# Expert outputs stored by indirect transfers of GpSimd instead of plain stores of SyncE, in a two-layer encoder trunk

## The chip, the cores and the metric

The kernel runs on one core of a Trainium2 chip. The metric is device time in microseconds (us) of one execution. Before the change it is 1436.44 us, the median of 3 runs (1435.87 to 1436.81). The trace shown here comes from one profiled execution that took 1436.07 us and whose instructions span 1434.3 us.

Engines by their short names: PE is TensorE, DVE VectorE, ACT ScalarE, POOL GpSimd, SP SyncE. SP, ACT and POOL also issue transfers. Transfers issued by SP go to DMA queue q1, those of POOL to queue q0, those of ACT to q10; all queues are served by the same 16 DMA engines.

## What is computed

Two layers. Each adds a token mixer to the residual, then a mixture of experts. Layer 0 mixes by a gated short convolution and a bidirectional RG-LRU behind one input projection, layer 1 by windowed attention. The part that the change touches is the mixture of experts (512 tokens, 1024 channels, 16 experts of width 512, 2 experts per token, all data float32):

```
def grouped_moe(h, router_w, router_bias, w_gate, w_up, w_down):
    scores = sigmoid(hf @ router_w)
    ...                       # best group of 4 experts, best 2 experts in it
    top_w = top_s / sum(top_s)
    slot_tok = full(cap, T).at[dest].set(tok)      # slots in blocks of 128 for one expert
    xs = hpad[slot_tok].reshape(n_blocks, 128, D)
    yb = (silu(xb @ w_gate[e]) * (xb @ w_up[e])) @ w_down[e]   # per block
    out = zeros(T + 1, D).at[slot_tok].add(yb * slot_w)
```

Each token takes 2 slots, so 1024 slots are taken in a layer. The in-projection of layer 0 is `z = h @ w_in`, 1024 by 2560.

## The kernel before

Every engine has its own hand-written list of instructions, joined by semaphores. There is no scheduler: what stands first in an engine's list runs first, and an instruction that waits holds up all behind it on that engine.

**In-projection of layer 0.** The weight is cut into five slabs of 128 x 8 x 512 (2 MB), loaded by SP with `load_in(g)`. PE makes 20 tiles of z, four per slab (`z_tile`). For slabs 1 to 4 the weight is split in two float32r parts: ACT copies half a slab (`high_in(g, half)`, line 800), DVE subtracts (`low_in`, line 1245), and PE multiplies (line 1743). Tiles 0 to 3 are copied by ACT from PSUM to one scratch tile, `u_in` (line 817), read by DVE's convolution `conv_b`. Tiles 4 to 11 are taken by ACT with `take_z` (line 829); both kinds count the semaphore `z_act`. Between them ACT runs the RG-LRU gates of four channel tiles j (lines 839 to 847), and DVE their products and scans (lines 1197 to 1213). ACT's order from j = 2 on is: gates, `take_z(9)`, square roots, `high_in(3, 0)`, then `take_z(10)` and the gates of j = 3.

Beside this, SP streams the modulation weights in slices of 512 KB through a ring of four (`load_mod`, line 426), which DVE sums (`mod_acc`, lines 1030 and 1032). SP's order in the middle of the stage is the rest of `load_mod(3)`, the slab `("out", 0)`, `load_in(3)`, `load_mod(4)`, `load_in(4)`.

**Memory for the experts' outputs.** `y_dram` has 23 blocks of 128 rows of 4 KB: 16 for the experts and 7 for blocks of experts that have over 128 tokens. The kernel before zeroes only the last 7, by POOL, early in the in-projection (lines 656 and 658).

**Expert stage, once per layer.** After routing, POOL gathers an expert's 128 token rows from `xn_dram` (lines 668 and 675), with an index column of `slot_tok`. An empty slot's index is past the bounds and its row is skipped. PE's step for expert e: first half of the gate product, transposes of the hidden rows of e - 1, second half, down product of e - 1 (line 1872), transposes of the input of e + 1 (line 1847), up product (lines 1861). DVE scales the down product of e - 1 into `ybuf` (`take_y`, line 1491), one of two buffers, and counts `yb_ready`. SP refills three weight slabs a step and then stores the whole `ybuf`, 128 rows, to `y_dram` (`store`, line 537). At the end come the blocks of experts with over 128 tokens (one in layer 0, two in layer 1, stored at line 576), and then POOL gathers every token's two rows of `y_dram` (line 719) and DVE adds them with their weights (`combine`).

Of the kernel before, what the change touches and what calls it, by code (L numbers as in the profile page):

```python
# [20 lines left out]
ALU = mybir.AluOpType  # L21
# [4 lines left out]
I32 = mybir.dt.int32  # L26
# [3 lines left out]
P = 128  # L30
# [4 lines left out]
HALF = 512  # L35
# [3 lines left out]
NE, NG, EPG = 16, 4, 4  # L39
FF = 512  # L40
FT = FF // P
MAX_OVER = 2 * S // P - 1
NBLK = NE + MAX_OVER
# [49 lines left out]
def build(nc, ctx, a, out):  # L93
    def small(name, shape, dt=F32):
        return ctx.enter_context(nc.sbuf_tensor(name, shape, dt))
# [28 lines left out]
    u_in = R[:, 0, :]  # L124
# [17 lines left out]
    ybuf = [R[:, 9:11, :].rearrange("p a n -> p (a n)"), R[:, 11:13, :].rearrange("p a n -> p (a n)")]  # L142
# [71 lines left out]
    empty = small("slot_empty", [P, WIDE])  # L214
    dst = small("dest", [P, 2, TT])
    info = small("over_info", [P, 8], I32)
    hot = small("hot_b", [P, TT, NE], BF16)
    idx = [small(f"gather_idx{i}", [P, 1], I32) for i in range(2)]

    xn_dram = nc.dram_tensor("xn_rows", [S, D], F32, kind="Internal").ap()  # L220
    y_dram = nc.dram_tensor("y_rows", [NBLK * P, D], F32, kind="Internal").ap()
# [24 lines left out]
    z_ready, z_act, z_dve = sem("z_ready"), sem("z_act"), sem("z_dve")  # L246
# [7 lines left out]
    xn_stored, place_ready, slots_summed, slots_ready = sem("xn_stored"), sem("place_ready"), sem("slots_summed"), sem("slots_ready")  # L254
# [160 lines left out]
    def _(sp):  # L415
# [94 lines left out]
        def stream_experts(l):  # L510
            e0 = l * NE

            free = {0: [(z_ready, 20), (mod_used, (MOD_SPLIT - 1) * MOD_SLICES + 4), (mod_used, MOD_SPLIT * MOD_SLICES), (y_ready, 8), (z_ready, 16), (y_ready, 8)],
                    1: [(av_ready, 8), (y_ready, 15), (y_ready, 16), (y_ready, 16), (y_ready, 16), (y_ready, 16)]}[l]
            for e in range(2):
                for c in range(3):
                    sp.wait_ge(*free[3 * e + c])
                    load_part(l, c, e, e)

            def refill(pair, par, more, first=False):  # L520

                e = 2 * pair + par
                if more:
                    sp.wait_ge(gate_done, e + (e0 + 1))
                    load_part(l, 0, e + 2, par)
                if not first:
                    sp.wait_ge(down_done, e + e0)
                    load_part(l, 2, e + 1, 1 - par)
                if more:
                    sp.wait_ge(up_done, e + (e0 + 1))  # L530
                    load_part(l, 1, e + 2, par)
                if not first:
                    store(e - 1, 1 - par)

            def store(e, par):
                sp.wait_ge(yb_ready, e + (e0 + 1))
                sp.dma_start(y_dram[bass.ds(e * P, P), :], ybuf[par]).then_inc(yb_stored[par], 16)

            refill(0, 0, True, first=True)
            refill(0, 1, True)  # L540
            with sp.Fori(1, NE // 2 - 1) as i:
                refill(i, 0, True)
                refill(i, 1, True)

            refill(NE // 2 - 1, 0, False)
            o = over[l]
            n_over = sp.value_load(info[0:1, 7:8], min_val=0, max_val=MAX_OVER)

            def load_over(k, name, c):
                ex = sp.value_load(info[0:1, bass.ds(k, 1)], min_val=0, max_val=NE - 1)  # L550
                sp.dma_start(part_dst(c, 0), part_src(l, c, ex)).then_inc(o[name], 16)

            sp.wait_ge(gate_done, e0 + NE - 1)
            sp.wait_ge(up_done, e0 + NE - 1)
            with sp.If(n_over > 0):
                load_over(0, "wg", 0)
                load_over(0, "wu", 1)
            sp.wait_ge(down_done, e0 + NE - 1)
            with sp.If(n_over > 0):
                load_over(0, "wd", 2)  # L560
                sp.sem_inc(o["stored"], 16)
            store(NE - 2, 0)
            if l == 0:
                for w, used in enumerate((gate_done, up_done, down_done)):
                    sp.wait_ge(used, e0 + NE)
                    load_slab(("qkv", w), w_qkv[:, :, w * HALF:(w + 1) * HALF])
            store(NE - 1, 1)
            with sp.Fori(0, MAX_OVER) as k:
                with sp.If(k + 1 < n_over):
                    ex = sp.value_load(info[0:1, bass.ds(k + 1, 1)], min_val=0, max_val=NE - 1)  # L570
                    for c, name, used in ((0, "wg", "gate"), (1, "wu", "gu"), (2, "wd", "down")):
                        sp.wait_ge(o[used], k + 1)
                        sp.dma_start(part_dst(c, 0), part_src(l, c, ex)).then_inc(o[name], 16)
                with sp.If(k < n_over):
                    sp.wait_ge(o["yb"], k + 1)
                    sp.dma_start(y_dram[bass.ds((k + NE) * P, P), :], ybuf[0]).then_inc(o["stored"], 16)
                    sp.wait_ge(o["stored"], (k + 2) * 16)
                    sp.sem_inc(turn_seen, 1)
            for par in range(2):
                sp.wait_ge(yb_stored[par], 16 * (NE // 2) * (l + 1))  # L580
# [32 lines left out]
    def _(gp):  # L613
# [18 lines left out]
        link(gp.iota(tok1[:, :], [[P, TT]], base=1, channel_multiplier=1, allow_small_or_imprecise_dtypes=True))  # L632
        link(gp.iota(b_id[:, :], [[1, WIDE]], base=0, channel_multiplier=0, allow_small_or_imprecise_dtypes=True))
        link(gp.iota(p_id[:, :], [[1, P]], base=0, channel_multiplier=0, allow_small_or_imprecise_dtypes=True))
        link(gp.memset(gpad[:, :, :], NEG))
        gp.sem_inc(consts_ready, 1)

# [19 lines left out]
        for b in range(NE, NBLK):  # L657
            gp.dma_start(y_dram[b * P:(b + 1) * P, :], zeros).then_inc(y_zeroed, 16)

        def gathers(l):  # L660
            e0 = l * NE
            gp.wait_ge(xn_ready, 4 * (2 * l + 2))
            link(gp.memset(R[:, 0:4, :], 0.0))
            gp.wait_ge(slots_ready, 2 * l + 1)
            gp.wait_ge(xn_stored, 16 * TT * (l + 1))

            def gather_first(buf, done):
# [9 lines left out]
                                      bounds_check=S - 1, oob_is_err=False).then_inc(done, 16)  # L677

            gather_first(0, xs_filled[0])
            gp.wait_ge(slots_ready, 2 * l + 2)  # L680
            gather_first(1, xs_filled[1])
            with gp.Fori(0, NE // 2 - 1) as i:
                link.enter_loop(i, 0, 2)
                for par in range(2):
                    gp.wait_ge(xs_turned, 2 * i + (par + e0 + 1))
                    gp.sem_inc(turn_seen, 1)
                    gather(2 * i + (par + 2), par, xs_filled[par])
                link.leave_loop(0, NE // 2 - 1)

            o = over[l]  # L690
            gp.wait_ge(route_ready, l + 1)
# [3 lines left out]
            def gather_over(k):  # L695
                gp.tensor_copy(idx[0][:, :], slot_tok[:, bass.ds(k + NE, 1)]).then_inc(o["step"], 1)
                gp.wait_ge(o["step"], k + 1)
                gp.sem_inc(turn_seen, 1)
                gp.indirect_dma_start(out=xs[0], out_offset=None, in_=xn_dram,
                                      in_offset=bass.IndirectOffsetOnAxis(ap=idx[0][:, 0:1], axis=0),  # L700
                                      bounds_check=S - 1, oob_is_err=False).then_inc(o["xs"], 16)

            with gp.If(n_over > 0):
                gather_over(0)
            with gp.Fori(0, MAX_OVER - 1) as k:
                with gp.If(k + 1 < n_over):
                    gp.wait_ge(o["turned"], k + 1)
                    gp.sem_inc(turn_seen, 1)
                    gather_over(k + 1)
# [309 lines left out]
    def _(v):  # L1019
# [337 lines left out]
        def place_first(l):  # L1357

            v.wait_ge(rank_ready, l + 1)
            link(stt(first_rank[:, :], hot[:, :, 0], -float(PAST), v3(ps[:, 1, 0:n])[:, :, 0], ALU.mult, ALU.add))  # L1360
            link(ts(first_rank[:, :], first_rank[:, :], float(PAST), None, ALU.add))
            tt_(first_hot, p_id[:, :].unsqueeze(1).to_broadcast([P, TT, P]), first_rank[:, :].unsqueeze(2).to_broadcast([P, TT, P]), ALU.is_equal).then_inc(place_ready, 1)
            v.wait_ge(slots_summed, 2 * l + 1)
            found = ps[:, 2, 0:1]
            link(ts(empty[:, 0:1], found, 0.0, float(NO_TOKEN), ALU.is_equal, ALU.mult))
            stt(slot_tok[:, 0:1], found, -1.0, empty[:, 0:1], ALU.add, ALU.add).then_inc(slots_ready, 1)
            v.wait_ge(slots_ready, 2 * l + 1)

        def route(l):

# [29 lines left out]
            slots = ps[:, 2, 1:WIDE]  # L1400
            link(ts(empty[:, 1:WIDE], slots, 0.0, float(NO_TOKEN), ALU.is_equal, ALU.mult))
            stt(slot_tok[:, 1:WIDE], slots, -1.0, empty[:, 1:WIDE], ALU.add, ALU.add).then_inc(slots_ready, 1)
            v.wait_ge(slots_ready, 2 * l + 2)

        def route_rest(l):

# [668 lines left out]
```

## Time and profile before

| | |
|---|---|
| median of 3 runs | 1436.44 us (1435.87 to 1436.81) |
| profiled execution | 1436.07 us, span 1434.3 us, mean granted PE clock 0.938 |
| PE busy | 1260.2 us, 88% of the span |
| DVE busy | 950.0 us, 66% |
| ACT busy | 616.9 us, 43% |
| POOL busy | 169.5 us, 12% |
| bytes moved | 353.14 MB, mean 246 GB/s |
| of these on queue q1 (SP) | 327.28 MB |
| of these on queue q0 (POOL) | 20.46 MB |

A share of busy time is a mean over stages with different limits, so the table alone does not say which engine sets the time at a given place. The chain of waits does: it starts at the last instruction and goes back, at each step, to what released it. A time in the views counts from the span's start.

### The profile page before, as it was taken

To read this page: it belongs to the slowest core of one execution; us is meant where nothing else is said; L and a number is where in the kernel's file an instruction comes from. 1 tells how busy PE (TensorE), PEld (TensorE's weight loads), DVE (VectorE), ACT (ScalarE), POOL (GpSimd) and SP (SyncE) were. 2 spreads that over 40 slices of the span, in tenths; PEclk is the share of its full clock that TensorE was granted. 3 is DMA by queue.
4 is the path that set the end of the run, shared out by engine and by line. 5 is a ranking of instruction groups with operands and counts; after the bars stand their busy time and mean duration, and the time that the engine had idled before them with its cause. 6 is when DMAs were issued, how large, how long until landed. Compare 5 with 4: busy or idle time off the path is not lost.

```text
span 1434.3 us, 14569 instructions
## 1 busy us (share of the span) xinstructions
PE 1260.2 (88%) x4997; PEld 853.9 (60%) x4997; DVE 950.0 (66%) x1331; ACT 616.9 (43%) x792; POOL 169.5 (12%) x177
## 2 busy tenths in 40 slices
PE   2999899948999999983999999999489999999881
PEld 2566665546666666741788854467367666667430
DVE  8678876467777777613866587856577777776114
ACT  3486301335555555402422167634255555554001
POOL 6100000010000000002000047710110000000002
PEclk9999899969999999997899999999599999999996
DMA  9836674257999999883375230023679999998445
GB/s 353 325 115 239 223 287 152 95 204 296 369 365 369 364 380 378 304 313 132 125 285 177 88 118 1 1 74 130 241 295 377 375 366 368 376 367 305 146 181 190
DMA packets 79552, 353.14 MB, mean 246 GB/s; under 512 B 12632, under 2 KB 12816, under 8 KB 70544
## 3 DMA queue, kind: packets, MB, share of 16 engines
q1 hardware_dynamic: 67616, 327.28, 61.7%
q0 software_dynamic: 8352, 20.46, 4.0%
q10 hardware_dynamic: 3536, 4.79, 0.9%
q8 instruction: 27, 0.44, 0.1%
q14 instruction: 21, 0.17, 0.0%
HBM read 334.15 MB, written 28.31 MB: 253 GB/s over the span
## 4 chain that ended last, share of the span: by engine, by line
PE 77%; DVE 11%; DMA 5%; ACT 3%; issue 3%; POOL 1%; SPq 0%; DVEq 0%; ACTq 0%; POOLq 0%
PE ps L1861 24%; PE ps L1872 17%; PE ps L1960 9%; PE ps L1781 4%; PE ps L1852 3%; PE ps L1743 3%; PE ps L1788 2%; PE ps L1847 2%; PE ps L1748 2%; DVE scratch L1032 2%; PE ps L2004 2%; PE ps L2032 2%; PE ps L2018 2%; DMA x_res<-in_x_dram 1%; PE ps L1866 1%
## 5 line engine op out<-in xcount | busy, mean ns | idle before, releaser
L1872 PE MATMUL ps<-slab_ring,scratch 128*128 128x512 f32 x560 | 246.5, 593 | 3.4 <-ACT scratch L940 2.1
L1861 PE MATMUL ps<-slab_ring_r,gate_rows_r 128*128 128x512 f32 x512 | 202.0, 394 | 0.0
L1872 PEld LDWEIGHTS ps<-slab_ring,scratch 128*128 128x128 f32 x560 | 105.8, 190 | 124.2 <-issue 117.3
L1453 DVE TENSOR_TENSOR slab_ring_r<-slab_ring,h_t_r 128x2048 fp32r<-128x2048 f32 x64 | 143.9, 2288 | 17.1 <-ACT h_t_r L862 17.1
L1960 PE MATMUL ps<-slab_ring_r 128*128 128x512 f32 x384 | 121.8, 399 | 1.8 <-DVE h_t_r L1089 1.8
L1861 PE MATMUL ps<-h_t_r,gate_rows_r 128*128 128x512 f32 x256 | 106.1, 414 | 14.8 <-DVE scratch_r L1487 7.6
L862 ACT ACTIVATE h_t_r<-slab_ring 128x2048 fp32r<-128x2048 f32 x64 | 118.7, 1902 | 0.0
L1861 PEld LDWEIGHTS ps<-slab_ring_r,gate_rows_r 128*128 128x128 f32 x512 | 98.2, 192 | 19.2 <-issue 0.5
L891 ACT ACTIVATE scratch<-ps,mod_ab 128x128 f32<-128x128 f32 x128 | 48.2, 457 | 136.2 <-PE ps L1847 136.2
L1861 PE MATMUL ps<-h_t_r,scratch_r 128*128 128x512 f32 x256 | 102.3, 400 | 0.0
L1453 DVE TENSOR_TENSOR slab_ring_r<-slab_ring,x_norm_r 128x2048 fp32r<-128x2048 f32 x32 | 73.3, 2293 | 41.3 <-ACT x_norm_r L862 41.3
L1453 DVE TENSOR_TENSOR slab_ring_r<-slab_ring,mod_ring_r 128x2048 fp32r<-128x2048 f32 x32 | 73.3, 2292 | 41.1 <-ACT mod_ring_r L862 41.1
L727 POOL TENSOR_SCALAR mod_ring<-mod_ring,row_rcp 128x512 f32<-128x512 f32 x48 | 77.0, 1616 | 185.7 <-DVE row_rcp L1634 185.7
L1960 PEld LDWEIGHTS ps<-slab_ring_r 128*128 128x128 f32 x384 | 72.8, 191 | 19.1 <-issue 2.9
L862 ACT ACTIVATE x_norm_r<-slab_ring 128x2048 fp32r<-128x2048 f32 x32 | 61.1, 1911 | 46.7 <-PE ps L1861 46.6
L862 ACT ACTIVATE mod_ring_r<-slab_ring 128x2048 fp32r<-128x2048 f32 x32 | 61.1, 1911 | 46.7 <-PE ps L1861 46.6
L1491 DVE TENSOR_TENSOR scratch<-ps,gate_rows 128x512 f32<-128x512 f32 x70 | 45.1, 686 | 53.9 <-PE ps L1872 53.0
L1743 PE MATMUL ps<-slab_ring_r,h_t_r 128*128 128x512 f32 x192 | 68.8, 436 | 9.7 <-DVE slab_ring_r L1245 9.7
L1960 PE MATMUL ps<-slab_ring_r,h_t_r 128*128 128x512 f32 x192 | 75.7, 395 | 0.0
L1032 DVE SCALAR_TENSOR_TENSOR scratch<-slab_ring,c_silu,scratch 128x1024 f32<-128x1024 f32 x49 | 69.1, 1410 | 3.8 <-DMA slab_ring<-in_mod_w_dram 2.2
L1861 PEld LDWEIGHTS ps<-h_t_r,gate_rows_r 128*128 128x128 f32 x256 | 49.8, 195 | 25.7 <-issue 16.4
L1743 PE MATMUL ps<-slab_ring_r 128*128 128x512 f32 x192 | 64.5, 415 | 0.0
(329 smaller groups left out, 2225.4 us busy)
## 6 DMA issues: line engine op xcount, KB each, us to landing
slab_ring<-in_expert_w_gate_dram SPq DMA_DIRECT2D x35, 2048.0 KB, 9.6
slab_ring<-in_expert_w_up_dram SPq DMA_DIRECT2D x35, 2048.0 KB, 10.1
slab_ring<-in_expert_w_down_dram SPq DMA_DIRECT2D x35, 2048.0 KB, 9.6
mod_ring<-in_mod_w_dram SPq DMA_DIRECT2D x40, 512.0 KB, 4.7
y_rows<-scratch SPq DMA_DIRECT2D x35, 512.0 KB, 10.2
slab_ring<-in_mod_w_dram SPq DMA_DIRECT2D x32, 512.0 KB, 4.7
slab_ring<-in_mod_w_dram SPq DMA_DIRECT2D x12, 1024.0 KB, 11.4
slab_ring<-in_w_qkv_dram SPq DMA_DIRECT2D x6, 2048.0 KB, 11.9
```

The costliest lines, as they stand in the source:

```text
L727: gp.tensor_scalar(prob[n % 8], prob[n % 8], rsum[:, n:n + 1], None, ALU.mult).then_inc(scaled_pool, 1)
L862: act.activation(top, w, ACT.Copy).then_inc(high_ready[c], 1)
L891: ins = act.activation(xsT[par][:, kt, :], ps[:, 0, kt * P:(kt + 1) * P], ACT.Identity, bias=AB[:, s, 1, kt:kt + 1], scale=AB[:, s, 0, kt: ...
L1032: ins = stt(dest, w, cs[:, m:m + 1], dest, ALU.mult, ALU.add)
L1453: tt_(rest, w, top.bitcast(F32), ALU.subtract).then_inc(low_ready[c], 1)
L1491: ins = tt_(buf[:, h * HALF:h * HALF + HALF], ps[:, 5 + h, :], G[:, 2 * l + 1, h * HALF:h * HALF + HALF], ALU.mult)
L1743: ins = pe.matmul(ps[:, z_bank(t), :], w[:, kt, cut], x[:, kt, :], start=(kt == 0 and i == 0), stop=(kt == KT - 1 and i == 2))
L1781: ins = pe.matmul(ps[:, 2 * t + half, :], mixT[:, kt, cut], slab(("out", half))[:, kt, :], start=(i == 0), stop=(i == KT - 1))
L1852: ins = pe.matmul(ps[:, bank, :], xsT[0][:, kt, :], w[:, kt, :], start=(kt == 0), stop=(kt == KT - 1))
L1861: ins = pe.matmul(ps[:, bank, :], x, w, start=(kt == 0 and i == 0), stop=(kt == KT - 1 and i == 2))
L1872: ins = pe.matmul(ps[:, 5 + h, :], hidT[:, f, :], w[:, 2 * f + h, :], start=(f == 0), stop=(f == FT - 1))
L1960: ins = pe.matmul(ps[:, i % 6, :], x[:, kt, cut], y[:, k, :], start=(kt == 0 and n == 0), stop=(kt == KT - 1 and n == 2))
```

## The change

Three things change.

POOL now also zeroes the 16 experts' blocks of `y_dram`, once, after its 7 old zero stores: it waits until `z_act` has reached 9 (the four copies to `u_in` and `take_z` of tiles 4 to 8), clears `u_in`, and issues 32 transfers of 128 rows x 2 KB (256 KB) from it. The expert stage of layer 0 begins only when all of them have landed.

The routing on DVE writes one more small tile, `y_slot`: the row number of each slot, or a number past the bounds for an empty slot. `slots_ready` counts three a layer instead of two, and POOL's second gather waits for the third.

SP's `store` is gone. POOL issues an indirect transfer of `ybuf` for each expert instead (`scatter`): a copy of one index column, then the transfer, in which the rows of empty slots are skipped. The stores of the extra blocks stay with SP.

```diff
@@ smalls
+    y_base = small("y_base", [P, NE])
+    y_slot = small("y_slot", [P, NE], I32)
+    y_idx = [small(f"store_idx{i}", [P, 1], I32) for i in range(2)]
@@ SP, stream_experts
-                if not first:
-                    store(e - 1, 1 - par)
-
-            def store(e, par):
-                sp.wait_ge(yb_ready, e + (e0 + 1))
-                sp.dma_start(y_dram[bass.ds(e * P, P), :], ybuf[par]).then_inc(yb_stored[par], 16)
...
-            store(NE - 2, 0)
...
-            store(NE - 1, 1)
@@ POOL, constants
+        link(gp.iota(y_base[:, :], [[P, NE]], base=0, channel_multiplier=1, allow_small_or_imprecise_dtypes=True))
@@ POOL, after the 7 old zero stores
+        gp.wait_ge(z_act, 9)
+        link(gp.memset(u_in, 0.0))
+        for b in range(NE):
+            for h in range(2):
+                gp.dma_start(y_dram[b * P:(b + 1) * P, h * HALF:(h + 1) * HALF], u_in).then_inc(y_zeroed, 16)
@@ POOL, gathers(l)
+            if l == 0:
+                gp.wait_ge(y_zeroed, 16 * (MAX_OVER + 2 * NE))
...
-            gp.wait_ge(slots_ready, 2 * l + 2)
+            gp.wait_ge(slots_ready, 3 * l + 3)
             gather_first(1, xs_filled[1])
-            with gp.Fori(0, NE // 2 - 1) as i:
-                link.enter_loop(i, 0, 2)
+
+            def scatter(e, ready, buf):
+                gp.wait_ge(yb_ready, ready)
+                gp.sem_inc(turn_seen, 1)
+                link(gp.tensor_copy(y_idx[buf][:, :], y_slot[:, bass.ds(e, 1)]))
+                gp.sem_inc(turn_seen, 1)
+                gp.indirect_dma_start(out=y_dram, out_offset=bass.IndirectOffsetOnAxis(ap=y_idx[buf][:, 0:1], axis=0), in_=ybuf[buf],
+                                      in_offset=None, bounds_check=NBLK * P - 1, oob_is_err=False).then_inc(yb_stored[buf], 16)
+
+            for par in range(2):
+                gp.wait_ge(xs_turned, par + e0 + 1)
+                gp.sem_inc(turn_seen, 1)
+                gather(par + 2, par, xs_filled[par])
+            with gp.Fori(1, NE // 2 - 1) as i:
+                link.enter_loop(i, 1, 4)
                 for par in range(2):
                     gp.wait_ge(xs_turned, 2 * i + (par + e0 + 1))
                     gp.sem_inc(turn_seen, 1)
                     gather(2 * i + (par + 2), par, xs_filled[par])
+                    scatter(2 * i + (par - 2), 2 * i + (par + e0 - 1), par)
...
+            scatter(NE - 4, e0 + NE - 3, 0)
@@ POOL, after the first gather of an extra block
+            for e in range(NE - 3, NE):
+                scatter(e, e0 + e + 1, e % 2)
@@ DVE, end of route(l)
+            tt_(y_slot[:, :], y_base[:, :], empty[:, 0:NE], ALU.add).then_inc(slots_ready, 1)
+            v.wait_ge(slots_ready, 3 * l + 3)
```

The list of POOL around the zero stores, in the kernel before (`x_norm` is the zeroed tile of the old stores, `scratch` in line 663 the buffers of the gathers):

```order
L656 MEMSET x_norm 128x1024 [waits pool_step,xn_turned]
L658 DMA y_rows<-x_norm 128x1024 [waits pool_step]
L658 DMA y_rows<-x_norm 128x1024 x6
L663 MEMSET scratch 128x2048 [waits xn_ready]
L668 DMA scratch<-xn_rows,slot_token 128x1024 [waits xn_stored,slots_ready,pool_step]
```

The same place in the changed kernel (`scratch` in lines 657 and 660 is `u_in`):

```order
L652 MEMSET x_norm 128x1024 [waits pool_step,xn_turned]
L654 DMA y_rows<-x_norm 128x1024 [waits pool_step]
L654 DMA y_rows<-x_norm 128x1024 x6
L657 MEMSET scratch 128x512 [waits z_act]
L660 DMA y_rows<-scratch 128x512 [waits pool_step]
L660 DMA y_rows<-scratch 128x512 x31
L667 MEMSET scratch 128x2048 [waits xn_ready,y_zeroed]
L672 DMA scratch<-xn_rows,slot_token 128x1024 [waits xn_stored,slots_ready,pool_step]
```

One memset and 32 transfers stand between the old zero stores and the first instruction of the expert stage.

The list of POOL in the loop over pairs of experts, changed kernel, the first expert of a pair:

```order
L677 ISA [waits xs_turned]
L677 COPY gather_idx<-slot_token 128x1
L70 ISA
L679 DMA scratch<-xn_rows,gather_idx 128x1024 [waits pool_step]
L688 REGISTER_ALU
L690 ISA [waits yb_ready]
L690 COPY store_idx<-y_slot 128x1
L70 REGISTER_ALU
L692 DMA y_rows<-scratch,store_idx 2944x1024 [waits pool_step]
```

The wait for `yb_ready` and the store stand behind the gather of the same step. SP's list in the same loop lost its wait for `yb_ready` and the store; before, it read:

```order
L445 DMA slab_ring<-in_expert_w_gate_dram 128x4096
L445 ISA [waits down_done]
L445 DMA slab_ring<-in_expert_w_down_dram 128x4x1024
L445 DMA slab_ring<-in_expert_w_up_dram 128x4096 [waits up_done]
L537 ISA [waits yb_ready]
L537 DMA y_rows<-scratch 128x1024
```

The three weight loads stay as they were and in the same order.

## Rows read from the trace of the kernel before

**Rows 1.** The chain that ended last: share of the span by engine.
```profile
PE 77%; DVE 11%; DMA 5%; ACT 3%; issue 3%; POOL 1%; SPq 0%; DVEq 0%; ACTq 0%; POOLq 0%
```

**Rows 2.** The same chain in time, one expert step: start us, us, what.
```profile
346.18 8.20 PE ps L1861 x36
...
354.82 2.75 PE ps L1861 x12
357.56 6.87 PE ps L1872 x16
365.32 8.20 PE ps L1861 x36
```

**Rows 3.** The same chain, in-projection.
```profile
119.96 1.30 DVE scratch L1032
...
122.12 15.00 DMA slab_ring<-in_w_in_ab_dram
137.17 1.79 issue
138.96 0.58 ACT x_norm L829
...
158.33 2.30 DVE slab_ring_r L1245
160.63 0.14 issue
160.77 13.95 PE ps L1743 x48
```

**Rows 4.** ACT in time, in-projection: start us, us, instruction [idle before <-releaser].
```profile
112.03 0.58 ACT L829 ACTIVATE x_norm<-ps 128x512 f32<-128x512 f32 x1
...
137.15 1.91 ACT L800 ACTIVATE h_t_r<-slab_ring 128x2048 fp32r<-128x2048 f32 x1 [7.40 <-DMA slab_ring<-in_w_in_ab_dram]
...
160.47 1.91 ACT L800 ACTIVATE h_t_r<-slab_ring 128x2048 fp32r<-128x2048 f32 x1 [7.12 <-DMA slab_ring<-in_w_in_ab_dram]
```

**Rows 5.** DVE in time, same stretch.
```profile
139.16 2.29 DVE L1245 TENSOR_TENSOR slab_ring_r<-slab_ring,h_t_r 128x2048 fp32r<-128x2048 f32 x1 [2.53 <-ACT h_t_r L800]
141.37 0.75 DVE L1030 TENSOR_SCALAR scratch<-mod_ring,c_silu 128x1024 f32<-128x1024 f32 x1
...
173.89 2.29 DVE L1245 TENSOR_TENSOR slab_ring_r<-slab_ring,h_t_r 128x2048 fp32r<-128x2048 f32 x1
```

**Rows 6.** SP's DMA issues in time, same stretch.
```profile
121.27 0.33 SPq L426 DMA_DIRECT2D mod_ring<-in_mod_w_dram  x1
121.64 0.43 SPq L417 DMA_DIRECT2D slab_ring<-in_w_out_ab_dram  x1
122.12 0.59 SPq L417 DMA_DIRECT2D slab_ring<-in_w_in_ab_dram  x1
```

**Rows 7.** DMA traffic of 112 to 118 us, then of 124 to 130 us.
```profile
DMA packets 411, 1.49 MB, mean 248 GB/s; under 512 B 48, under 2 KB 48, under 8 KB 411
...
DMA packets 1163, 2.39 MB, mean 398 GB/s; under 512 B 32, under 2 KB 32, under 8 KB 1163
```

**Rows 8.** POOL in time: its memset and seven zero stores.
```profile
41.09 0.95 POOL L656 MEMSET x_norm<- 128x1024 f32 x1 [15.49 <-PE ps L1712]
42.36 3.93 POOL L658 DMA_DIRECT2D y_rows<-x_norm  x7 [0.32 <-POOL x_norm L656]
```

**Rows 9.** DMA queues of 48 to 54 us (packets, MB, share), and a load issued there.
```profile
q0 software_dynamic: 312, 1.15, 50.5%
q1 hardware_dynamic: 321, 1.18, 50.3%
...
slab_ring<-in_w_in_ab_dram SPq DMA_DIRECT2D x1, 2048.0 KB, 18.4
```

**Rows 10.** The same kind of load, issued in 148 to 154 us.
```profile
slab_ring<-in_w_in_ab_dram SPq DMA_DIRECT2D x1, 2048.0 KB, 8.6
```

**Rows 11.** POOL in time: gathers in the expert loop, then two later transfer issues.
```profile
346.44 0.18 POOL L673 COPY gather_idx<-slot_token 128x1 int32 x1 [22.72 <-PE ps L1847]
347.48 1.02 POOL L675 DMA_INDIRECT scratch<-xn_rows,gather_idx  x1 [0.85 <-POOL gather_idx L673]
365.57 0.19 POOL L673 COPY gather_idx<-slot_token 128x1 int32 x1 [17.07 <-PE ps L1847]
...
666.46 1.89 POOL L719 DMA_INDIRECT mod_ring<-y_rows,y_row  x1 [0.30 <-issue]
```

**Rows 12.** All stores of line 537: duration ns, first and last start us.
```profile
L537 SPq DMA_DIRECT2D y_rows<-scratch x32: 342/356/1792, 352.1 to 1346.5; - x32
```

**Rows 13.** DVE in time, end of the routing of layer 0.
```profile
307.79 0.18 DVE L1402 SCALAR_TENSOR_TENSOR slot_token<-ps,slot_empty 128x23 int32<-128x23 f32 x1
309.39 1.36 DVE L1481 TENSOR_SCALAR scratch<-ps,mod_ab 128x128 f32<-128x128 f32 x4 [1.42 <-PE ps L1847]
```

More of the change, by code:

```diff
@@ L658, in _ @@
             gp.dma_start(y_dram[b * P:(b + 1) * P, :], zeros).then_inc(y_zeroed, 16)
+        gp.wait_ge(z_act, 9)
[3 more added lines that the diff above has]
+                gp.dma_start(y_dram[b * P:(b + 1) * P, h * HALF:(h + 1) * HALF], u_in).then_inc(y_zeroed, 16)
         def gathers(l):
             e0 = l * NE
+            if l == 0:
+                gp.wait_ge(y_zeroed, 16 * (MAX_OVER + 2 * NE))
             gp.wait_ge(xn_ready, 4 * (2 * l + 2))
             link(gp.memset(R[:, 0:4, :], 0.0))
-            gp.wait_ge(slots_ready, 2 * l + 1)
+            gp.wait_ge(slots_ready, 3 * l + 1)
             gp.wait_ge(xn_stored, 16 * TT * (l + 1))
@@ L687, in gathers @@
                     gather(2 * i + (par + 2), par, xs_filled[par])
-                link.leave_loop(0, NE // 2 - 1)
+                    scatter(2 * i + (par - 2), 2 * i + (par + e0 - 1), par)
+                link.leave_loop(1, NE // 2 - 1)
+            scatter(NE - 4, e0 + NE - 3, 0)
             o = over[l]
@@ L1366, in place_first @@
             stt(slot_tok[:, 0:1], found, -1.0, empty[:, 0:1], ALU.add, ALU.add).then_inc(slots_ready, 1)
-            v.wait_ge(slots_ready, 2 * l + 1)
+            v.wait_ge(slots_ready, 3 * l + 1)
         def route(l):
@@ L1402, in route @@
             stt(slot_tok[:, 1:WIDE], slots, -1.0, empty[:, 1:WIDE], ALU.add, ALU.add).then_inc(slots_ready, 1)
-            v.wait_ge(slots_ready, 2 * l + 2)
+            tt_(y_slot[:, :], y_base[:, :], empty[:, 0:NE], ALU.add).then_inc(slots_ready, 1)
+            v.wait_ge(slots_ready, 3 * l + 3)
         def route_rest(l):
```

## Prediction

> **What bounds the kernel now.** I read the chain of waits first, by engine: PE holds 77% of it, DMA 5% [rows 1]. In time, the expert loop is PE alone: a step goes from 346.18 to 365.32 us, 19.1 us, and in it the chain names only PE lines [rows 2]. No transfer, not the weights and not the stores of line 537, stands in the chain there. 14 steps of each layer look like this. So what the change takes off the DMA engines in the loop pays only if something waits for them, and nothing does.
>
> Then I read the stage into which the new zero stores are put. Here a transfer does stand in the chain: slab 3 of the in-projection is issued at 122.12 us, and the chain waits 15.00 us for it [rows 3]. ACT sat idle for 7.40 us before its copy of that slab at 137.15 us [rows 4]. ACT runs in order, so `take_z(10)` (138.96 us) and the gates of j = 3 stand behind that copy; behind these come DVE's scans, DVE's second split of slab 3 at 158.33 us, and PE's tiles at 160.77 us, from which PE runs on [rows 3]. DVE waited 2.53 us for the same copy [rows 5]. Nothing on this path has slack: if slab 3 lands later, all of it moves.
>
> **The zero stores: when.** `take_z(8)` is ACT's row at 112.03 us, 0.58 us long, so `z_act` is 9 at 112.6 us [rows 4]. A memset of 128x1024 took 0.95 us and the first store followed 0.3 us later [rows 8]; half the size makes about 0.5 us, so the first zero store is issued at 113.5 us. Seven stores took 3.93 us to issue, 0.56 us each [rows 8]; 32 take 18 us, until 131.5 us. They carry 32 x 0.262 = 8.39 MB. Issued at 0.47 MB a us, they come faster than the 0.39 to 0.40 MB a us that the DMA engines move when full (398 GB/s [rows 7]), so q0 has a backlog throughout.
>
> **What a backlog on q0 does to q1.** The trace of before shows it once, while the seven old zero stores run: from 48 to 54 us q0 moved 312 packets and q1 321, each for half of the engines' time [rows 9]. So the queues take turns packet by packet. A 2 MB slab issued then took 18.4 us to land [rows 9]; one issued at 151.8 us, with q0 empty, took 8.6 us [rows 10].
>
> The Trainium skill, page "DMA: Bandwidth & Descriptors", section "Where 436 GB/s comes from", gives about 358 GB/s as the limit between HBM and one core's SBUF. The trace shows 398 GB/s with loads alone. By the page's figure the same bytes as below would cost 4.45 / 0.358 = 12.4 us, 1.3 us more than I take.
>
> **The sum.** By 121.27 us, when slab 3's group of loads begins [rows 6], the DMA engines can move 7.8 us x 0.40 = 3.1 MB; q1 has about 1.0 of the 1.49 MB of its 112 to 118 us left to move [rows 7], so 2.1 MB of zeros are done and 6.3 MB wait. Ahead of slab 3's landing, q1 has a modulation slice (0.52 MB), the slab `("out", 0)` (2.10 MB) and slab 3 itself (2.10 MB) [rows 6], 4.7 MB: at 0.39 MB a us that is 12.1 us, and with some 3 us of start and landing it is the 15.9 us from 121.27 to 137.15. So q1 is near first in, first out. Turn by turn, each 2 KB packet of the two slabs lets one 2 KB packet of zeros pass (4.19 MB) and each 4 KB packet of the slice one of 2 KB (0.26 MB): 4.45 MB, less than the 6.3 MB that wait. At 0.40 MB a us: **+11.1 us** on the landing of slab 3, from 137.1 to about 148 us, and on everything behind.
>
> Bounds of this term: if the zeros that wait all go first, 6.3 / 0.39 = 16.2 us. If POOL issues as slowly as its slowest issue in the trace, 1.89 us [rows 11], zeros come at 0.262 / 1.89 = 0.139 MB a us; q1 then has 0.26 MB a us and its 4.7 MB take 18.1 instead of 12.1 us: +6.0 us. I take 11.1, which rests on the nearest rows, the same kind of store by the same engine in the same stage [rows 8, 9].
>
> After slab 3 has landed, about 1.9 MB of zeros are left, beside the four slices that follow. The first three of these are needed at 141.37, 142.1 and 143.4 us plus 11 [rows 5]: 1.57 MB of slices and 0.8 MB of zeros take 5.9 us from the slab's last packet at about 146.3 us, and with 2 us of landing the third slice is there at 154.2, needed at 154.5: nothing. The zeros end near 157 us. Slab 4, issued at 151.8 us before, is issued 11 us later too, at 163, with q0 empty again. Its copy on ACT (160.47 us [rows 4]) feeds a DVE instruction at 173.89 us [rows 5], 11.5 us of slack after the copy's 1.91 us. Both slabs together therefore cost one delay. The expert stage's new wait for all zero stores is over more than 130 us before POOL reaches it: its first gather is near 300 us, hidden by the rest of the in-projection and the out-projection.
>
> **The loop.** SP loses 32 issues of 0.36 us [rows 12] and q1 loses 32 x 0.52 = 16.8 MB; at most 8.4 MB come back on q0, since of a layer's 2048 rows at most 1024 are taken. Worth nothing where PE alone is in the chain. POOL gains per step a copy (0.18 us), 0.85 us and an issue of 1.02 us, as its gather costs [rows 11]: 2.1 us out of 17.07 us idle. The new wait for `yb_ready` stands behind the gather of the same step. Only the next gather is queued behind it, 19 us later, and the awaited count is reached before: `take_y(e - 2)` follows the down product that PE does just before the transposes that release the gather. If that cover were gone, 2.1 us x 28 would be the price. `ybuf` is needed again two steps later, 38 us, against a landing of some 10 us. Nothing.
>
> **Routing.** One DVE instruction of about 0.18 us behind the row at 307.79; DVE then idles 1.42 us for PE [rows 13]. It delays POOL's second gather by 0.2 us, whose rows PE needs 11 us later. Nothing, in either layer. In the tails the stores of experts 14 and 15 were and are out of the chain; the last extra block's store and the gathers that follow are unchanged.
>
> Sum: 1436.07 + 11.1 = **1447.2 us** for the profiled execution; the median of before is 0.37 us above that execution, within its runs' spread of 0.94 us.
>
> **The rivals.**
>
> A, POOL's issue is slow. The Trainium skill, page "DMA: Bandwidth & Descriptors", section "SWDGE vs HWDGE vs iDMA", says that GpSimd writes its descriptors to SBUF and is locked out while VectorE is in a two-port mode. The mechanism in rows: 1.89 us an issue instead of 0.56 [rows 8, 11], with DVE nearly full in 113 to 131 us. The price is the lower bound above, +6.0 us, 1442.1. Against it: the seven stores beside a busy DVE took 0.56 us each.
>
> B, more than turn by turn. The zeros that wait go first (+16.2), or the slices behind slab 3 come late and DVE waits for them too: 1449.5 to 1453. For it: 2 KB writes to HBM at this density are in no row.
>
> C, hidden anyway. SP's loads are served first, or slab 3's delay stays under 3 us: 1436 to 1439. Against it: the half and half of [rows 9].
>
> D, the other side. The loop waits for DMA in a way that the chain does not name, and fewer bytes help. If the loop were bound by bytes, 8.4 MB less at 0.37 MB a us would give 22.7 us back, which against 11.1 makes 1424.5. It decides from 11.1 / 28 = 0.4 us a step. Against it: every step is 19.1 us, all on PE, with no idle time named [rows 2].
>
> That the rows of empty slots are moved after all would not matter, as nothing waits for the loop's stores.
>
> **How the numbers follow.** Forecast 0.62 (own range 1444.5 to 1449.5), A 0.14, B 0.12, C 0.09, D 0.03. A measurement of this kernel can tell 0.2%, 2.9 us, from no change. Slower by more than that: forecast, A and B, 0.88. Within: C, 0.09. Faster: D, 0.03. The range 1441 to 1452.5 takes in A and most of B and leaves out C, D and the end of B.
>
> **What would show it.** ACT's copy of slab 3 starts near 148 us instead of 137.15, with some 18 us idle before it on the transfer. From 113.5 us q0 and q1 share the DMA engines near 1:1 in packets until about 157 us. PE's tile row of 160.77 us stands near 172, and the offset then stays at 11 us to the end. The expert step is still 19.1 us. If slab 3 lands before 141 us, the term is wrong. If the offset grows or shrinks after 172 us, I have missed a wait or a gain; if a step of the loop changes by over 0.1 us, the loop was not PE's alone.

## Result: 0.94% slower, and the profile after

| | before | changed |
|---|---|---|
| median of 4 runs, same chip | 1436.15 us (1434.85 to 1436.81) | 1448.95 us (1448.75 to 1451.38) |
| ratio | | 1.0094 (95% interval 1.0082 to 1.0107) |
| profiled execution, its span | 1436.07, 1434.3 us | 1449.06, 1447.3 us |
| bytes moved | 353.14 MB | 353.04 MB |
| of these on q1 (SP) | 327.28 MB | 310.50 MB |
| of these on q0 (POOL) | 20.46 MB | 37.14 MB |

The forecast was 1447.2 us, range 1441 to 1452.5. The bytes moved are the same before and after, within 0.1 MB: 16.8 MB of full stores left q1, and 8.4 MB of zeros and 8.3 MB of indirect stores came to q0.

The chain of waits of the changed kernel, in-projection (start us, us, what; it answers to [rows 3]; lines of the changed kernel are some 20 higher):

```profile
122.91 27.79 DMA slab_ring<-in_w_in_ab_dram
...
152.54 0.58 ACT x_norm L850
...
171.90 2.30 DVE slab_ring_r L1266
174.20 0.14 issue
174.34 13.84 PE ps L1765 x48
```

Slab 3 was 27.8 us in flight instead of 15.0, and every row behind it stands 13.6 us later: `take_z(10)` at 152.54 instead of 138.96, PE's tiles at 174.34 instead of 160.77. ACT in time shows the wait itself (to be laid beside [rows 4]), and DVE's row beside that of [rows 5]:

```profile
150.72 1.91 ACT L821 ACTIVATE h_t_r<-slab_ring 128x2048 fp32r<-128x2048 f32 x1 [21.10 <-DMA slab_ring<-in_w_in_ab_dram]
...
174.05 1.91 ACT L821 ACTIVATE h_t_r<-slab_ring 128x2048 fp32r<-128x2048 f32 x1 [7.13 <-DMA slab_ring<-in_w_in_ab_dram]
```

```profile
152.74 2.29 DVE L1266 TENSOR_TENSOR slab_ring_r<-slab_ring,h_t_r 128x2048 fp32r<-128x2048 f32 x1 [14.82 <-ACT h_t_r L821]
```

The wait for slab 3 grew from 7.40 to 21.10 us. The wait for slab 4, in the second row, stayed at 7.1 us, since it was issued that much later too. POOL in time shows the zero stores (compare [rows 8]):

```profile
112.54 0.53 POOL L657 MEMSET scratch<- 128x512 f32 x1 [66.09 <-ACT x_norm L850]
113.36 11.20 POOL L660 DMA_DIRECT2D y_rows<-scratch  x21 [0.30 <-POOL scratch L657]
138.94 5.87 POOL L660 DMA_DIRECT2D y_rows<-scratch  x11 [14.37 <-issue]
```

The first is issued at 113.36 us, 0.53 us each, but POOL stops for 14.37 us after the 21st. And the traffic while slab 3 was under way, from 121.5 us to its landing at 150.7 us (packets, MB, share):

```profile
q1 hardware_dynamic: 2601, 6.12, 53.8%
q0 software_dynamic: 1634, 5.36, 49.1%
```

5.36 MB of zeros passed. In the kernel before, q1 moved 5.54 MB in its 15.6 us of that kind, alone. The two shares near one half are a mean over four unlike stretches, in each of which the engines were full:

| stretch, us | q0: packets, MB | q1: packets, MB | what happens |
|---|---|---|---|
| 121.5 to 126 | 481, 1.57 | 5, 0.02 | zeros alone |
| 126 to 135.4 | 628, 2.04 | 668, 1.59 | turns |
| 135.4 to 142.6 | 26, 0.07 | 1384, 2.81 | loads alone, after POOL's pause |
| 142.6 to 150.7 | 499, 1.68 | 544, 1.71 | turns |

The expert loop, in the chain (it answers to [rows 2]):

```profile
359.43 8.20 PE ps L1883 x36
368.06 2.77 PE ps L1883 x12
370.83 6.87 PE ps L1894 x16
378.59 8.20 PE ps L1883 x36
```

A step is 19.16 us, as before. The indirect stores beside it, and POOL in time:

```profile
L692 POOL DMA_INDIRECT y_rows<-scratch,store_idx x32: 971/1026/1909, 362.9 to 1360.9; - x32
...
DMA to landing us min/median/max: 3.2/9.3/11.9
```

```profile
359.70 0.18 POOL L677 COPY gather_idx<-slot_token 128x1 int32 x1 [22.77 <-PE ps L1869]
360.74 1.02 POOL L679 DMA_INDIRECT scratch<-xn_rows,gather_idx  x1 [0.86 <-POOL gather_idx L677]
361.76 0.20 POOL L690 COPY store_idx<-y_slot 128x1 int32 x1
362.92 1.02 POOL L692 DMA_INDIRECT y_rows<-scratch,store_idx  x1 [0.96 <-POOL store_idx L690]
```

They land within 11.9 us, against 38 us until `ybuf` is needed again.

### The profile page after: what moved, and what is told of

Same layout as the page of the kernel before. It is cut to its first block, busy times and chain, and to the rows that moved or that the text cites. A ratio compares the mean times of both kernels' runs of the same rounds, so it can differ in the third digit from the quotient of the medians.

```text
span 1447.3 us, 14737 instructions
## 1 busy us (share of the span) xinstructions
PE 1259.5 (87%) x4997; PEld 852.2 (59%) x4997; DVE 945.3 (65%) x1333; ACT 616.6 (43%) x792; POOL 245.5 (17%) x275
## 2 busy tenths in 40 slices
DMA packets 82113, 353.04 MB, mean 244 GB/s; under 512 B 15220, under 2 KB 15404, under 8 KB 73104
## 3 DMA queue, kind: packets, MB, share of 16 engines
q1 hardware_dynamic: 63008, 310.50, 57.8%
q0 software_dynamic: 15520, 37.14, 7.0%
## 4 chain that ended last, share of the span: by engine, by line
PE 77%; DVE 10%; DMA 6%; ACT 3%; issue 2%; POOL 1%; SPq 0%; DVEq 0%; POOLq 0%; ACTq 0%
PE ps L1883 24%; PE ps L1894 17%; PE ps L1982 8%; PE ps L1765 4%; PE ps L1803 4%; PE ps L1874 3%; PE ps L1810 2%; PE ps L1869 2%; PE ps L1770 2%; DMA slab_ring<-in_w_in_ab_dram 2%; PE ps L2026 2%; PE ps L2054 2%; PE ps L2040 2%; DVE scratch L1053 2%; DMA x_res<-in_x_dram 1%
## 5 line engine op out<-in xcount | busy, mean ns | idle before, releaser
L1982 PE MATMUL ps<-slab_ring_r 128*128 128x512 f32 x384 | 121.1, 397 | 2.9 <-DVE h_t_r L1110 2.9
L677 POOL COPY gather_idx<-slot_token 128x1 int32 (+1 forms) x28 | 5.2, 185 | 377.1 <-PE ps L1869 377.1
```

The costliest lines, as they stand in the source:

```text
L1982: ins = pe.matmul(ps[:, i % 6, :], x[:, kt, cut], y[:, k, :], start=(kt == 0 and n == 0), stop=(kt == KT - 1 and n == 2))
```

## The experiments

Two theories go through all of them. T: the cost is slab 3's later landing, because zeros on q0 and loads on q1 take turns at the DMA engines. S: part of it comes from the indirect stores or the routing. Others are named where they enter. Each ratio is to runs of the kernel before on the same chip.

**e2, the zeros without the rest.** The kernel before, with POOL's memset, its 32 stores and the wait for them; SP still stores the outputs.

```diff
+        gp.wait_ge(z_act, 9)
+        link(gp.memset(u_in, 0.0))
+        ...                       # 32 stores, as in the change
         def gathers(l):
+            if l == 0:
+                gp.wait_ge(y_zeroed, 16 * (MAX_OVER + 2 * NE))
```

> The kernel before plus the 32 zero stores at the changed kernel's place; SP still stores the outputs. Theory T (the zeros cost all, by taking turns with slab 3's load): 1449, within 1.5 us of the changed kernel, ACT's copy of slab 3 near 150.7 us. Rival S (part of the 13 us comes from the indirect stores or the routing): below 1447.

Measured 1450.98 us, ratio 1.0093 (1.0077 to 1.0108), the changed kernel's own ratio. The zeros alone make the whole cost; S falls.

**e3, the rest without the cost of the zeros.**

```diff
-        gp.wait_ge(z_act, 9)
+        gp.wait_ge(z_ready, 20)
```

> The changed kernel with the zero stores held until the last tile of the in-projection (z_ready 20, some 205 us), where the DMA engines are half idle. Theory T: the delay is gone, 1436.2 within 1.5 us; this is then also what the indirect stores alone are worth, nothing. Rival D (fewer bytes in the expert loop help): 1433 or less. Rival S: above 1438.

Measured 1436.75 us against 1437.00, ratio 0.9995 (0.9986 to 1.0004). ACT's copy of slab 3 is back:

```profile
137.15 1.91 ACT L821 ACTIVATE h_t_r<-slab_ring 128x2048 fp32r<-128x2048 f32 x1 [7.14 <-DMA slab_ring<-in_w_in_ab_dram]
```

So the place makes the cost: the same 8.4 MB cost nothing here. The indirect stores are worth nothing that can be measured, in either direction, to within some 0.1%.

**e4, the zeros earlier.** They begin when the last convolution has read `u_in`, 35 us sooner.

```diff
-        gp.wait_ge(z_act, 9)
+        gp.wait_ge(y_zeroed, 16 * MAX_OVER)
+        gp.wait_ge(xr_ready, LRU_TILES)
```

> The changed kernel with the zero stores begun as soon as the last convolution has read u_in (xr_ready 4, some 77.5 us), 35 us earlier. DMA engines moved about 140 GB/s from 80 to 120 us before, so 8.4 MB fit before slab 3's loads at 121 us, POOL's pause included. Theory T: 1436 to 1438. If the cost were tied to the stores and not to slab 3: 1449.

Measured 1436.54 us against 1435.68, ratio 1.0004 (0.9995 to 1.0014), as T has it. POOL's pause of 14.43 us after 21 stores is there as well and costs nothing.

**e5, the zeros just behind slab 3.**

```diff
-        gp.wait_ge(z_act, 9)
+        gp.wait_ge(weight_high, 5)
```

> The changed kernel with the zero stores held until ACT has copied the first half of slab 3 (some 139 us, 26 us later than in the changed kernel). The backlog then meets slab 4, which has 11.5 us of slack. Theory T (turns): slab 4 lands 6 to 7 us later, inside the slack: 1436 to 1438.5. Rival V (zeros that wait go first): slab 4 lands 14 us later, 1439 or more.

Measured 1439.67 us, ratio 1.0022 (1.0012 to 1.0032). Slab 4 did as T says: its copy starts at 167.56 instead of 160.47 us, 7.1 us later and not 14, inside its slack. So V falls here, though the time alone would fit it:

```profile
167.56 1.92 ACT L821 ACTIVATE h_t_r<-slab_ring 128x2048 fp32r<-128x2048 f32 x1 [14.27 <-DMA slab_ring<-in_w_in_ab_dram]
```

The time lies above T's range all the same, for a reason that neither theory had. DVE waits for modulation slices:

```profile
168.91 0.75 DVE L1051 TENSOR_SCALAR scratch<-mod_ring,c_silu 128x1024 f32<-128x1024 f32 x1 [1.34 <-DMA mod_ring<-in_mod_w_dram]
170.87 1.29 DVE L1053 SCALAR_TENSOR_TENSOR scratch<-mod_ring,c_silu,scratch 128x1024 f32<-128x1024 f32 x1 [1.21 <-DMA mod_ring<-in_mod_w_dram]
173.22 1.28 DVE L1053 SCALAR_TENSOR_TENSOR scratch<-mod_ring,c_silu,scratch 128x1024 f32<-128x1024 f32 x1 [1.06 <-DMA mod_ring<-in_mod_w_dram]
```

These three add to 3.6 us, and the chain of this run goes through such a slice (issued at 163.11 us, 10.0 us in flight). I had given slack to slab 4 and none of my attention to the slices that stand behind it in q1.

**e6, half the dose.**

```diff
         for b in range(NE):
+            if b == NE // 2:
+                gp.wait_ge(z_ready, 20)
             for h in range(2):
```

> The changed kernel with 16 of the 32 zero stores at their place and 16 held until 205 us. About 2 of the 4.2 MB are moved before slab 3's group of loads begins; the rest passes before slab 3 lands, by T and V alike: 2.1 / 0.40 = 5 us, 1441.5. If the cost came from POOL's pause in issuing (it stopped after 21 of 32) and not from bytes, it would be gone: 1436.

Measured 1440.69 us, ratio 1.0029 (1.0017 to 1.0040). Slab 3's copy starts at 142.83 us, 5.7 us late, with no pause among the 16 stores at that place; the span is 3.7 us longer than before, less than the 5 expected, so 2 us were regained behind it. The cost is there without a pause beside slab 3, so it does not come from the pause.

**e8, twice the dose.**

```diff
-        for b in range(NE):
+        for b in list(range(NE)) * 2:
```

> The changed kernel with the zeroing done twice, 64 stores instead of 32, all at the same place. Theory T (turns while slab 3 loads): slab 3 lands at most some 2 us later than in the changed kernel, and slab 4 is slowed inside its slack: 1449 to 1453. Rival V (all zeros that wait go first): 14.7 MB ahead of slab 3, 1470 or more.

Measured 1450.99 us, ratio 1.0102 (1.0076 to 1.0127). Slab 3's copy starts at 152.40 us, 1.7 us later than in the changed kernel, for 8.4 MB more. Two things bound the delay. POOL pauses after the same 21 stores, so most of the added zeros are not yet issued while slab 3 loads; the 14.7 MB of the expectation could not stand ahead of it. And from 142.6 us on, when zeros are issued again, the queues take turns (635 packets on q0 and 645 on q1 until 152.4 us). Had the 28 stores that POOL issues from 138.29 us on gone first, their 7.3 MB at 0.41 MB a us would have held slab 3 up by some 18 us, by my estimate. So zeros first (V), part of rival B, falls for loads that are already under way. For the start of the loads it does not: see the part on the prediction.

**e9, half the descriptor memory.**

```diff
-    nc = _bacc.Bacc("TRN2", target_bir_lowering=False, num_devices=1, dynamic_dma_scratch_size=4096)
+    nc = _bacc.Bacc("TRN2", target_bir_lowering=False, num_devices=1, dynamic_dma_scratch_size=2048)
```

> The changed kernel with half the memory for POOL's transfer descriptors (2048 instead of 4096). If the pause after 21 stores is the full descriptor memory (28 stores with the 7 old ones, 9 descriptors a store and DMA engine, 252 of 256), POOL now pauses after 7 of the 32 (14 with the old ones). Fewer zeros wait when slab 3's loads begin: by T 1440 to 1447. If the pause has another cause, it stays after 21 and the time at 1449.

Measured 1445.47 us, ratio 1.0067 (1.0051 to 1.0084). POOL pauses as expected, and slab 3's copy starts at 146.44 us:

```profile
113.93 3.75 POOL L660 DMA_DIRECT2D y_rows<-scratch  x7 [0.30 <-POOL scratch L657]
124.20 7.63 POOL L660 DMA_DIRECT2D y_rows<-scratch  x14 [6.52 <-issue]
146.01 6.04 POOL L660 DMA_DIRECT2D y_rows<-scratch  x11 [14.19 <-issue]
```

The doses give one line. The MB are those of q0 from 121.5 us to the start of slab 3's copy:

| | zeros that passed | slab 3's copy later by | MB a us |
|---|---|---|---|
| e6, half | 2.39 MB | 5.7 us | 0.42 |
| e9, half the descriptor memory | 3.85 MB | 9.3 us | 0.41 |
| changed kernel | 5.36 MB | 13.6 us | 0.39 |
| e2, zeros alone | 5.90 MB | 14.6 us | 0.41 |
| e8, double | 6.15 MB | 15.3 us | 0.40 |

A megabyte of zeros in slab 3's way costs 2.4 to 2.5 us, whatever changes the number of megabytes. (The stage begins up to 0.7 us later in some of these runs than in the kernel before; with that taken off it is 2.3 to 2.6 us.) The last column is the rate of full DMA engines, 0.40 MB a us. So the line says that bytes in the way make the delay; it does not say by what rule the queues share.

**e10, slab 3 out of the way of the zeros.** The changed kernel, with SP's order altered:

```diff
-        load_mod(3)
-        sp.wait_ge(z_ready, 4)
-        load_slab(("out", 0), w_out[:, :, 0:HALF])
+        load_mod(3, range(6))
         sp.wait_ge(z_ready, 8)
         load_in(3)
+        load_mod(3, range(6, MOD_SLICES))
+        load_slab(("out", 0), w_out[:, :, 0:HALF])
         load_mod(4)
```

> The changed kernel with SP's load of slab 3 moved ahead of the last two modulation slices of that group and of the slab of the out-projection, issued near 113 us instead of 122. Theory T (only slab 3's landing carries the cost): it lands by 126 us, before ACT is free for it at 129.7, so the cost of the zeros goes and the 7.4 us that the kernel before waited go too: 1429 to 1433. Rival W (the zeros also delay the modulation slices that DVE needs, or slab 4): 1436 or more.

Measured 1439.65 us, ratio 1.0023 (1.0010 to 1.0036), the time of W. ACT starts slab 3's copy at 129.93 us without a wait, so slab 3 carries nothing any more, and 9 of the 13 us against the kernel before are gone. But DVE now waits for its slices:

```profile
130.22 1.28 DVE L1053 SCALAR_TENSOR_TENSOR scratch<-mod_ring,c_silu,scratch 128x1024 f32<-128x1024 f32 x1 [1.62 <-DMA mod_ring<-in_mod_w_dram]
132.54 1.28 DVE L1053 SCALAR_TENSOR_TENSOR scratch<-mod_ring,c_silu,scratch 128x1024 f32<-128x1024 f32 x1 [1.04 <-DMA mod_ring<-in_mod_w_dram]
...
145.83 0.75 DVE L1051 TENSOR_SCALAR scratch<-mod_ring,c_silu 128x1024 f32<-128x1024 f32 x1 [4.00 <-DMA mod_ring<-in_mod_w_dram]
```

T in its strict form (slab 3 alone) falls. The slices are a second carrier (7.9 us of DVE's waiting in this stage), largely covered by slab 3's own delay in the changed kernel. This run also shows the queues' turns at their plainest, from 130 to 140 us:

```profile
q0 software_dynamic: 756, 2.47, 61.2%
q1 hardware_dynamic: 754, 1.62, 41.6%
```

The packets are equal in number. The bytes and the time are not.

**e11 and e12, the same move without the zeros in the way.** e11 is the kernel before with e10's edit. e12 is e3 with it.

> The kernel before with SP's load of slab 3 moved ahead of two modulation slices and of the slab of the out-projection, nothing else. If slab 3's landing alone holds this stretch, the 7.4 us that ACT waited go: 1429. If DVE is next behind it (it idled 5.65 us from 130 to 150 us), at most 5.6 us go, and the slices that now come later may take some back: 1431 to 1434. If the stretch is held by something else: 1436.

> The same move of slab 3's load in the changed kernel with the zero stores held until some 205 us: indirect stores, zeros out of the way, slab 3 early. If the indirect stores are worth nothing either way, it is equal to the kernel before with that move, within 1.5 us. If fewer bytes in the expert loop help once the in-projection is shorter, it is below it.

Measured 1433.48 us (ratio 0.9983, 0.9974 to 0.9992) and 1433.09 us (0.9980, 0.9970 to 0.9989), against 1435.92 us. Both are faster than before by 2.4 to 2.8 us. ACT no longer waits for slab 3, yet only a third of the 7.4 us is gained, at the lower edge of what the DVE case allowed. In e11 ACT's next gates begin at 136.17 us instead of 139.56, 3.4 us sooner, and now wait for DVE's work on j = 2:

```profile
136.17 1.28 ACT L839 ACT_TABLE_LOAD   x1 [3.88 <-DVEq L1212]
```

No wait of DVE for a slice is left in e11. e10, the same move with the zeros in the way, is some 6 us slower: that is what the zeros cost once slab 3 is out of their way. Two waits grew between e11 and e10, DVE's for slices from nothing to 7.9 us and ACT's for slab 4 from 7.0 to 11.9 us; how the 6 us divide between them is not shown. e12 beside e11 repeats e3's finding on a shorter in-projection: 0.4 us apart, inside the intervals.

## Why the prediction was right, and where it was off

The place, the sign and the way in which the delay passes on were right. The size of the delay came near in part by luck, as two errors one way met one the other way. The loop gave nothing (19.16 us a step), the routing's instruction was hidden, the wait for all zeros was long over, and the delay passed on in full: 13.6 us at slab 3's copy, 13.0 at the end. The offset shrinks in small steps: 13.57 us at PE's row of 174.34 us, 13.35 at 218.8 us, 12.84 at the start of layer 1's projection. What makes these steps is not shown.

**The time of the zero stores** was predicted at 113.5 us and 0.56 us each; it was 113.36 and 0.53. The pause after 21 was not foreseen.

**The term that was mis-sized** is the zeros that pass while slab 3 is loaded: 4.45 MB predicted, 5.36 MB measured, at 0.39 MB a us, so 13.6 instead of 11.1 us. The sum let the queues take turns from 121.27 us until slab 3 had landed, 2 KB for 2 KB. The stretches in the section on the result show three differences.

First, the loads began late, as the records of single packets show. Issued from 121.16 us on, their first packet moves at 124.97 us; in the kernel before it moved at 122.23, 1.0 us after its issue. Until 126 us the engines moved 1.57 MB of zeros and 0.02 MB of loads. To this extent rival B's "zeros that wait go first" was true. What holds the loads back there stays open; in e9, where POOL's earlier pause had nearly drained q0, the first packet comes at 122.67 us, no later than before the change, as this run's stage is 0.4 us later.

Second, a turn of q0 was larger. Where both queues have work, their packets do alternate, as predicted (756 to 754 in e10). But the 80 packets of a zero store (10,912 on q0 in e2, less 8,352 before, over 32 stores) are 64 of 4 KB and 16 without data, so two of its 128 rows of 2 KB go in one packet, while the slabs' packets carry 2 KB. In those 10 us of e10 q0 moved 2.47 MB to q1's 1.62. [rows 9] could not show this: there the packets of both queues carry 3.7 KB on average, so that turns by packet, by bytes and by time look alike.

Third, and the other way, POOL's pause took the zeros away. From 135.4 to 142.6 us q0 moved 0.07 MB. The last 11 stores hold 2.88 MB, of which 1.68 MB passed before slab 3's copy; with no pause up to 1.2 MB more could have passed, by my estimate 3 us more. The pause lessened the cost.

A smaller one: I took q1's work until slab 3's landing as 4.7 MB. It moved 6.12 MB, since slices issued behind slab 3 shared its way. They did so before the change too, where q1 moved 5.54 MB; only the 0.6 MB between the two came with the zeros. The predicted sign, near 1:1 in packets until about 157 us, holds in the stretches of turns and not over the whole (1634 to 2601).

**After slab 3**: the third slice was predicted there 0.3 us before its need. DVE waited 1.8 us in two pieces for slices in this stage, 0.3 before. The sum hardly shows it, but e5 and e10 show the same wait with slab 3's delay taken away, 4.2 and 7.9 us in all. That margin was too thin to be called nothing.

**Rivals.** A: POOL's issues stayed at 0.53 us; the lock-out that the Trainium skill names, page "DMA: Bandwidth & Descriptors", section "SWDGE vs HWDGE vs iDMA", is not seen in these rows. B: its queue jumping fell with e5 and e8, but for the first 4 us; its late slices are real but small here. C, a delay under 3 us, fell with the result. D fell with e3 and with e12 beside e11. The Trainium skill's 358 GB/s between HBM and one core (same page, "Where 436 GB/s comes from") would have given an estimate of 12.4 us on my bytes, nearer to 13.6, for a wrong reason: the traffic ran at 394 GB/s over those 29.2 us.

## What to carry to other kernels

A transfer that nobody waits for still costs time, if it shares the DMA engines with one that the chain names: here 2.4 to 2.5 us a megabyte, up to the bytes that fit in while the awaited load is in flight, and the same 8.4 MB cost nothing 35 us earlier or 90 us later. So place bulk traffic by the chain and the bandwidth of each stretch, and then look for the second load behind the first, since its wait is hidden until the first is cured. Bytes saved in a loop that is bound by PE bought nothing here. And if two queues share the engines, look at the size of a packet on each before you reckon with turns.

## What the runs showed of the hardware

**When POOL pauses.** POOL stops issuing when 28 of the direct stores have been issued since the start, even if the early ones have long landed. The 7 old stores land by about 63 us, and the 21st new one is still the last before the pause in the changed kernel, in e2 to e5 and in e8. In e6 it is the same 28th, 16 stores at 113 us and 5 at 210 us. In e8 the next pause comes after a further 28. With half the descriptor memory it is the 14th, and the next comes after a further 14. So the count goes with the memory. That the memory is reused only once it is full is my inference.

**When it goes on.** These pauses last 6.5 to 27 us, and the end of each is in the trace's packet records: in all 12 pauses of the ten runs that have zero stores, POOL issues again 0.85 to 1.1 us after the last packet of q0 has been moved (changed kernel: 137.85 and 138.94 us; e9: 123.35 and 124.20, then 145.15 and 146.01). So in these runs it went on only once its queue was empty, not when the next store had landed. The pause was longest, 27.2 us, in e3 and e12, where q0 emptied latest.

**How two queues share.** While both have work they alternate packet by packet (756 to 754 in e10). A packet of zeros carried 4 KB and took 160 ns of a DMA engine, one of the loads mostly 2 KB and 90 ns, hence 61% to 42% of the time.
